# The expert stage of a hybrid decoder layer: one stream of expert pairs becomes two streams that share the array

## What is computed

```python
def hier_moe(h, w_group, b_group, w_router, b_router, w_gate, w_up, w_down):
    pg = softmax(hf @ w_group + b_group)               # 4 groups
    g_val, g_idx = lax.top_k(pg, 1)                    # the best group
    pe = softmax(logits of the 8 experts of that group)
    e_val, e_idx = lax.top_k(pe, 2)                    # its two best experts
    combine = one_hot(expert) * g_val * e_val / sum(e_val)
    a = einsum('btd,edf->btef', h, w_gate)             # w_gate, w_up: 32 x 1024 x 256, f32
    u = einsum('btd,edf->btef', h, w_up)
    z = silu(a) * u * combine
    return einsum('btef,efd->btd', z, w_down)          # w_down: 32 x 256 x 1024, f32
```

## Time and profile before

| | us |
|---|---|
| three runs | 690.07, 686.41, 688.15; median 688.15 |
| span of the profiled execution (its own time beside it isn't given) | 683.7 |
| TensorE matmul busy | 543.3 (79%) |
| TensorE weight loads busy | 274.8 (40%) |
| VectorE busy | 230.6 (34%) |
| GpSimd busy | 178.0 (26%) |
| ScalarE busy | 151.6 (22%) |
| DMA, mean over the span | 247 GB/s |

### The profile page before, as it was taken

One profiled execution on the slowest core, in us unless ns is written; L12 is line 12 of the kernel. 1 busy time (PEld: TensorE's weight loads), 2 busy tenths in 40 slices (PEclk: granted clock), 3 DMA queues, 4 the chain that ended last, 5 costly groups with the idle time before them and its releaser, 6 DMA issues.

```text
span 683.7 us, 7215 instructions
## 1 busy us (share of the span) xinstructions
PE 543.3 (79%) x2420; PEld 274.8 (40%) x2421; DVE 230.6 (34%) x530; ACT 151.6 (22%) x312; POOL 178.0 (26%) x204
## 2 busy tenths in 40 slices
PE   2639999999988799954049989989999979789470
PEld 1328777787534344313023333333333323233120
DVE  0421444232494477785301111111111101011295
ACT  1211444624565012211011111111111101011021
POOL 4200001000543464364531112112212111111075
PEclk9959999999899899986559999999999989999785
DMA  8991855500846802107649976539999999995611
GB/s 288 387 384 30 271 215 185 184 5 6 299 205 230 309 22 105 61 4 275 278 145 402 424 303 247 202 117 417 420 419 420 420 419 420 417 379 198 251 53 73
DMA packets 46005, 168.98 MB, mean 247 GB/s; under 512 B 13178, under 2 KB 22450, under 8 KB 30590
## 3 DMA queue, kind: packets, MB, share of 16 engines
q1 hardware_dynamic: 36682, 146.48, 54.8%
q0 software_dynamic: 8944, 21.87, 9.0%
q10 hardware_dynamic: 340, 0.09, 0.1%
HBM read 165.18 MB, written 18.32 MB: 268 GB/s over the span
## 4 chain that ended last, share of the span: by engine, by line
PE 57%; DVE 13%; DMA 12%; SPq 8%; issue 5%; ACT 3%; POOL 1%; POOLq 0%; DVEq 0%
PE B L1663 16%; PE B L1415 15%; PE B L1682 7%; DMA wex<-in_w_up 4%; DMA win<-in_w_in 3%; PE B L1579 3%; PE B L1352 3%; SPq L369 3%; SPq L371 2%; SPq L368 2%; PE B L1484 2%; DVE bn L1139 2%; DMA ada<-in_w_ada 2%; DVE yy L1321 1%; PE B L1644 1%
## 5 line engine op out<-in xcount | busy, mean ns | idle before, releaser
L1663 PE MATMUL B<-wex,XT 128*64 128x512 f32 x640 | 152.1, 625 | 18.0 <-DMA wex<-in_w_up 10.0
L1415 PE MATMUL B<-hT,win 128*128 128x256 f32 (+1 forms) x448 | 103.1, 390 | 8.1 <-DMA win<-in_w_in 8.1
L1663 PEld LDWEIGHTS B<-wex,XT 128*64 128x64 f32 x640 | 53.2, 144 | 114.8 <-issue 113.6
L1415 PEld LDWEIGHTS B<-hT,win 128*128 128x128 f32 x448 | 85.6, 193 | 28.2 <-DMA win<-in_w_in 8.6
L1682 PE MATMUL B<-wex,zT 128*64 128x512 f32 x320 | 73.1, 599 | 0.6
L1294 DVE TENSOR_TENSOR z<-silu_g,B 128x256 f32<-128x256 f32 x20 | 8.4, 421 | 162.8 <-ACT silu_g L852 162.8
L621 POOL COPY sidx<-idx_all 128x1 int32 (+1 forms) x20 | 3.6, 181 | 200.7 <-DVE yo L1299 200.7
L1579 PE MATMUL B<-wout,yT 128*128 128x512 f32 x112 | 51.3, 617 | 0.0
L1644 PE MATMUL B<-ident,X 128*128 128x128 f32 x168 | 28.4, 295 | 26.8 <-DMA X<-h_dram,gidx 26.8
L852 ACT ACTIVATE silu_g<-B 128x256 f32<-128x256 f32 x20 | 7.7, 384 | 154.7 <-PE B L1663 154.7
L1299 DVE COPY yo<-B 128x512 f32<-128x512 f32 x20 | 13.8, 692 | 83.1 <-PE B L1682 83.1
(11 more groups left out here) (320 smaller groups left out, 627.9 us busy)
## 6 DMA issues: line engine op xcount, KB each, us to landing
wex<-in_w_gate SPq DMA_DIRECT2D x32, 1024.0 KB, 16.7
wex<-in_w_up SPq DMA_DIRECT2D x32, 1024.0 KB, 19.4
wex<-in_w_down SPq DMA_DIRECT2D x32, 1024.0 KB, 20.8
ada<-in_w_ada SPq DMA_DIRECT2D x12, 1024.0 KB, 9.6
ada<-in_w_ada POOLq DMA_DIRECT2D x12, 1024.0 KB, 7.0
win<-in_w_in SPq DMA_DIRECT2D x7, 1024.0 KB, 13.1
wout<-in_w_out SPq DMA_DIRECT2D x1, 4096.0 KB, 13.4
yy<-y_dram SPq DMA_DIRECT2D x8, 512.0 KB, 6.7
```

The lines of the kernel that those rows point to most:

```text
L1415: last = pe.matmul(B[(q % 2) * 2 + h][:, 0:cn], win[:, n % 3, k, col:col + P], hT[:, k, c0:c0 + cn], start=(k == 0), stop=(k == KD - 1))
L1663: last = pe.matmul(B[2 + j % 2][64 * q:64 * q + 64, :], XT[:, j % 2, k, 64 * q:64 * q + 64], gu[:, :, k, :], start=(k == 0), stop=(k == KD ...
```

## The change

The 32 experts are split into two streams that share each step. Stream A has the experts 0 to 7 one at a time, with WA = 64 rows of one expert in a step; stream B has the other 24 in 12 pairs, with WB = 32 rows of each of the two. A step has one unit of A (an expert) and one of B (a pair), and each stream advances with step counts of its own (`uend`, two scans instead of one). The number of steps is the larger of the two sums; a stream that has ended stays at its last unit with empty rows. The array works in four quarters of 128x32: two with A's expert and its rows 0 to 31 and 32 to 63, two with the pair of B. With the counts above, A's experts take 1 1 1 1 3 2 3 2 steps (14), and B's pairs 1 1 1 1 1 2 2 2 1 1 1 1 (15).

Each stream has two places for its weights (`wA0`, `wA1`; `wB0`, `wB1`), so TensorE has four arms for a step instead of three, `arm = 2 * (A's unit odd) + (B's unit odd)`, and each has twice the products of f32 data in quarters (32 for gate/up, 16 for down). TensorE's code of a turn is written out once instead of three times, in one loop over all TURNS (now 11, as MAXSTEP is 44), and each step has an `If` of its own. ScalarE, VectorE and GpSimd keep the three forms, with the `If` per step in the last. SP's loop over pairs becomes a list written out by hand (LOADS). Before the steps, A0, A1 are loaded early, B0 after the stores of x1, then B1.

VectorE's arithmetic for slots, places and needs grows by some operations (64 or 32 rows per step, depending on the stream). GpSimd makes the numbers of steps as one row instead of a grid. The needs of the semaphores and the final waits of GpSimd follow.

Cut to its core (the rest is the arithmetic of slots on VectorE, and the same `one(i, j, ...)` with its `If` on the other engines):

```diff
-CAP = 64
-NPAIR = NE // 2
-
-MAXSTEP = (2 * NT + (CAP - 1) * NPAIR) // CAP
+NA, NB = EPG, (NE - EPG) // 2
+NU = NA + NB
+WA, WB = 64, 32
+
+MAXSTEP = max((2 * NT + (WA - 1) * NA) // WA, (2 * NT + (WB - 1) * NB) // WB)
 RING = 4
 AHEAD = RING - 1
 TURNS = (MAXSTEP + RING - 1) // RING
-MINTURNS = NPAIR // RING
+MINTURNS = max(NA, NB) // RING
...
-        SETS = 3
-        wex = [row("wex0", [P, 2, EXW], "r", 0), row("wex1", [P, 2, EXW], "r", 8 * EXW), row("wex2", [P, 2, EXW], "x", 0)]
+        wA = [row("wA0", [P, 1, EXW], "r", 0), row("wA1", [P, 1, EXW], "r", 4 * EXW)]
+        wB = [row("wB0", [P, 2, EXW], "x", 0), row("wB1", [P, 2, EXW], "r", 8 * EXW)]
...
+        LOADS = [("A", 2), ("B", 2), ("A", 3), ("B", 3), ("B", 4), ("A", 4), ("B", 5), ("A", 5), ("B", 6), ("B", 7),
+                 ("A", 6), ("B", 8), ("A", 7), ("B", 9), ("B", 10), ("B", 11)]
...
-            for q in range(2):
-                load_expert(q, 0, q)
+            for i in range(2):
+                load_a(i)
...
-            sp.wait_ge(lgT_ps, 2)
-            load_expert(2, 1, 0)
+            sp.wait_ge(x1_stored, 16 * (TT + 1))
+            load_b(0, 0)
+            load_b(0, 1)
             sp.wait_ge(lg_ps, 1)
             sp.wait_ge(h2_stored[0], 16 * (TT // 2 + 1))
             sp.wait_ge(h2_stored[1], 16 * (TT // 2))
-            load_expert(3, 1, 1)
-
-            sp.wait_ge(x1_stored, 16 * (TT + 1))
-            load_expert(4, 2, 0, (True, False))
+            load_b(1, 0)
             sp.wait_ge(X_in[AHEAD - 1], 16)
...
+            load_b(1, 1)
...
+            for kind, i in LOADS:
+                before = (i - 2) if kind == "A" else NA + i - 2
+                last_step = sp.value_load(uend_i[0:1, before:before + 1], min_val=1, max_val=MAXSTEP)
                 for half, done in enumerate((gu_ps, y_ps)):
                     sp.wait_ge(done, last_step)
-                    for q in range(2):
-                        load_expert(2 * SETS * i + (2 * j + q), j, q, (half == 0, half == 1))
-
-            with sp.Fori(1, NPAIR // SETS) as i:
-                for j in range(SETS):
-                    load_pair(i, j)
-            for j in range(NPAIR % SETS):
-                load_pair(NPAIR // SETS, j)
-
-            last_step = sp.value_load(pend_i[0:1, NPAIR - 2:NPAIR - 1], min_val=1, max_val=MAXSTEP)
+                    parts = (half == 0, half == 1)
+                    if kind == "A":
+                        load_a(i, parts)
+                    else:
+                        load_b(i, 0, parts)
+                        load_b(i, 1, parts)
...
-            def turn(i, peeled):
-
-
-                for j in range(RING):
-                    n = RING * i + j
-                    place = pe.value_load(place_i[0:1, bass.ds(n, 1)], min_val=0, max_val=SETS - 1)
-                    need = pe.value_load(wneed[0:1, 0, bass.ds(n, 1)], min_val=64, max_val=64 * NPAIR)
-                    need_down = pe.value_load(wneed[0:1, 1, bass.ds(n, 1)], min_val=80, max_val=32 * NPAIR + 48)
-                    for pl in range(SETS):
-                        with pe.If(place == pl):
+            def lanes(a, b):
+
+                return [wA[a][:, 0, :], wA[a][:, 0, :], wB[b][:, 0, :], wB[b][:, 1, :]]
+
+            def one(i, j):
+                n = RING * i + j
+                arm = pe.value_load(arm_i[0:1, bass.ds(n, 1)], min_val=0, max_val=3)
+                need_a = pe.value_load(wneed[0:1, 0, bass.ds(n, 1)], min_val=32, max_val=16 * NA)
+                need_b = pe.value_load(wneed[0:1, 1, bass.ds(n, 1)], min_val=64, max_val=32 * NB)
+                for a in range(2):
+                    for b in range(2):
+                        with pe.If(arm == 2 * a + b):
                             pe.wait_ge(XT_v, n + 1)
                             pe.wait_ge(XT_a, n + 1)
-                            pe.wait_ge(w_in[pl], need)
+                            pe.wait_ge(wA_in[a], need_a + ADA)
+                            pe.wait_ge(wB_in[b], need_b + ADA)
                             for k in range(KD):
-                                for q in range(2):
-                                    gu = wex[pl][:, q, 0:GU].rearrange("p (c k f) -> p c k f", c=2, k=KD)
-                                    last = pe.matmul(B[2 + j % 2][64 * q:64 * q + 64, :], XT[:, j % 2, k, 64 * q:64 * q + 64],
+                                for g, w in enumerate(lanes(a, b)):
+                                    gu = w[:, 0:GU].rearrange("p (c k f) -> p c k f", c=2, k=KD)
+                                    last = pe.matmul(B[2 + j % 2][32 * g:32 * g + 32, :], XT[:, j % 2, k, 32 * g:32 * g + 32],
                                                      gu[:, :, k, :], start=(k == 0), stop=(k == KD - 1))
                             last.then_inc(gu_ps, 1)
                             pe.wait_ge(X_in[(j + 1) % RING], 16 * i + 16 + (16 if j == RING - 1 else 0))
@@ -1671,29 +1703,27 @@
                             last.then_inc(zT_ps, 1)
                             transpose_X((j + 1) % RING, i, 1)
                             pe.wait_ge(zT_ready, n + 1)
-                            if not (peeled and j == 0):
-                                pe.wait_ge(y_v, n)
-                                pe.wait_ge(y_a, n)
-                            pe.wait_ge(down_in[pl], need_down)
+                            pe.wait_ge(y_v, n + 1)
+                            pe.wait_ge(y_a, n + 1)
+                            pe.wait_ge(dA_in[a], need_a)
+                            pe.wait_ge(dB_in[b], need_b)
                             for k in range(2):
                                 for c in range(2):
-                                    for q in range(2):
-                                        dn = GU + k * D + c * 512
-                                        last = pe.matmul(B[5 + c][64 * q:64 * q + 64, :], zT[:, k, 64 * q:64 * q + 64],
-                                                         wex[pl][:, q, dn:dn + 512], start=(k == 0), stop=(k == 1))
+                                    dn = GU + k * D + c * 512
+                                    for g, w in enumerate(lanes(a, b)):
+                                        last = pe.matmul(B[5 + c][32 * g:32 * g + 32, :], zT[:, k, 32 * g:32 * g + 32],
+                                                         w[:, dn:dn + 512], start=(k == 0), stop=(k == 1))
                             last.then_inc(y_ps, 1)
 
             pe.wait_ge(steps_ready, 1)
             pe.wait_ge(X_in[0], 16)
             transpose_X(0, 0, 0)
             transpose_X(0, 0, 1)
-            turn(0, True)
-            with pe.Fori(1, MINTURNS) as i:
-                turn(i, False)
-            nturns = pe.value_load(turns[0:1, 0:1], min_val=MINTURNS, max_val=TURNS)
-            with pe.Fori(MINTURNS, TURNS) as i:
-                with pe.If(nturns > i):
-                    turn(i, False)
+            nsteps = pe.value_load(steps_i[0:1, 0:1], min_val=RING * MINTURNS, max_val=MAXSTEP)
+            with pe.Fori(0, TURNS) as i:
+                for j in range(RING):
+                    with pe.If(nsteps > RING * i + j):
+                        one(i, j)
 
```

More of the change, by code:

```diff
@@ L846, in copy_XT, with one @@
                 act.activation(XT[:, s % 2, 4:8, :], B[1][:, :].rearrange("p (k m) -> p k m", m=P), ACT.Copy).then_inc(XT_a, 1)
-            def turn(i, peeled):
-                for j in range(RING):
-                    n = RING * i + j
[L851 to L865, removed]
+            def one(i, j, first):
+                n = RING * i + j
+                act.wait_ge(gu_ps, n + 1)
+                act.activation(silu_g[:, :], B[2 + j % 2][:, 0:DE], ACT.Silu).then_inc(silu_done, 1)
+                act.wait_ge(zT_ps, n + 1)
+                act.activation(zT[:, :, :], B[4][:, 0:2 * P].rearrange("p (k m) -> p k m", m=P), ACT.Copy).then_inc(zT_ready, 1)
+                copy_XT(j + 1, n + 1)
+                act.wait_ge(y_ps, n + 1)
+                if not first:
+                    act.wait_ge(y_out[j], 16 * i)
+                act.activation(yo[:, j, 512:D], B[6][:, :], ACT.Copy).then_inc(y_a, 1)
+            copy_XT(0, 0)
+            for j in range(RING):
+                one(0, j, True)
+            with act.Fori(1, MINTURNS) as i:
+                for j in range(RING):
+                    one(i, j, False)
+            nsteps = act.value_load(steps_i[0:1, 0:1], min_val=RING * MINTURNS, max_val=MAXSTEP)
             with act.Fori(MINTURNS, TURNS) as i:
-                with act.If(nturns > i):
-                    turn(i, False)
+                for j in range(RING):
+                    with act.If(nsteps > RING * i + j):
+                        one(i, j, False)
             def xhat2(t, n):
@@ L1240, in _ @@
[L1240 to L1244 removed]
+            step(dve.tensor_scalar(unum_i[:, 0, 0:NA], B[5][:, 0:NA], 1.0, float(WA - 1), ALU.max, ALU.add))
+            link(dve.tensor_reduce(umax[:, NA:NU], B[5][:, NA:NE].rearrange("p (a b) -> p a b", b=2), AX.X, ALU.max))
@@ L1276, in _ @@
```

(25 more changed lines are left out.)

187 lines of the change are left out of this document (94 added, 93 removed).

## The result

The changed kernel takes 988.29 us (median of 4 runs, 985.90 to 990.72) where the kernel before takes 687.28 us (4 runs, 686.30 to 690.07): 1.4385 times the time, 95% interval 1.4339 to 1.443, so 301 us slower. Forecast were 859 us and at most 940.

The account below looks back on a forecast made before the run. The prediction saw TensorE's array as busiest, with DMA full from about 460 to 605 us. Span 683.7 + 58 (stage) + 112 (exit) + 1 (VectorE) = 855 us, with 4.5 us to the median 859 us; range 690 to 940 us.

Parts of the forecast that it names:

- the 8 blocks taken as what is held: TensorE's code store: 128 KiB in blocks of 16 KiB, so 8 blocks stay and the new 14.6-block turn does not.
- The jumps back: TensorE's turn loop: on each of three jumps back the first block is fetched again, 15 us in all.
- The walk along the loads alone: Expert stage timed by the weight loads and their gates, without other effects: steps 3, 4, 5 late, end at 607 us.
- Hidden are about 2.6 us, the down product of 3.65 us less its issue: Skipped arms between steps: 2.6 us of each code-fetch wait is covered by the down product.
- I take 5.0: Skipped arms between steps: each block not held costs 5.0 us, chosen between 3.4 and 5.8; 111 us in all.
- at 3.4 us (the queues are empty then) that is 126 us: TensorE leaving its loop: 37 places not held at 3.4 us each, 126 us, of which 112 us show.
- packets in pairs less than 2 us apart: Sign in TensorE's code queue that the prediction is wrong, because code is fetched ahead.
- The other engines' bodies are a few instructions per step: nothing.: Leaving the loop on engines other than TensorE: no added time.
- That the code stays: Rival: TensorE holds 15 blocks or more, only turn 1 pays; 664 to 675 us, 15 in 100.
- That the exit costs nothing: Rival: chains of arms cost, but exit jumps reach blocks that stay; 747 us, 12 in 100.
- fetching ahead of the jumps: Rival: several blocks fetched at once, chains cost a third and the exit half; about 750 us, 8 in 100.
- Tiles that don't overlap: Rival: four narrow array tiles don't overlap, each step 10.7 us longer, 160 us; 2 in 100.

Follow-up runs that it names:

- the step written once: The changed kernel with TensorE's exit edit, plus its step written once instead of four times and single XT and gate/up bank: 681.25 us.
- pairs, 20 steps: The kernel before, 687.28 us; where code doesn't stay, the same with 96 never-executed array instructions added to each arm, 820.24 us.
- exit of TensorE mended: The changed kernel with one more comparison around all four steps of a turn in TensorE's loop: 817.53 us.
- the one with reversed arms: The changed kernel with TensorE's exit edit, plus the four arms written in reverse order in every second step: 809.67 us.
- the last kernel: The kernel with TensorE's step written once, plus one comparison per turn on the other three engines and GpSimd's final counts read before its last loop: 669.82 us.

## Why the prediction was right and wrong

**Right.** The mechanism: code that doesn't stay, arms skipped in series, an exit through far jumps. A table of four kernels shows the first of these, in us (those of the right column are single runs, and the step written once also differs in its single XT):

| | code stays | code doesn't stay |
|---|---|---|
| pairs, 20 steps | 687 | 820 |
| two streams, 15 steps, exit of TensorE mended | 681 | 818 |

Right were also the 8 blocks taken as what is held, the order of the gaps (0.30 us where no arm is skipped, 25 us where six are), over 100 packets, the step's body (12.7 us: 398.2 us of stage less 177.8 of gaps and 30.4 of lower clock, by 15), the narrow tiles, B0's arrival, and that slow steps cover the loads. The jumps back were priced at 5 us each; against the means by skipped arms, the six of the kernel after and the one with reversed arms cost from 1.3 us less to 12.2 more, 5.3 on average. The walk along the loads alone, 607 us, is near the 613.9 us of the last kernel, where code costs least, and in part that is luck. It has the late weights of steps 4 and 5 (413 and 441 us, measured 421.5 and 447.9). From step 5 to step 15 both take 152 us, but the walk by 12.5 us a step and 27 us of waits for weights, the kernel by steps of 15.2 us on average with no such wait.

**Wrong: sizes.** The sum missed the span by 132 us, in two halves.

- *The stage*, forecast to end at 690 us, ended at 755.7. The terms that failed are "Hidden are about 2.6 us, the down product of 3.65 us less its issue" and, less, "I take 5.0". The prediction has 28.5 blocks for the skips, 3 for the jumps back and one late block inside an arm, 32.5 at about 5 us, less 2.6 us in each of 12 gaps: 131 us (111, 15 and 5). The trace has 177.8 us of gaps with 33 packets in them. So the count held; a block cost 5.4 us, 13 us more in all; and the 31 us of cover weren't there. In the first gap five packets make 25.19 us, with nothing left to take off. Six skipped arms were 25.2 and 27.8 us where the prediction has 19.4, four 13.0 to 15.9 (10.4), three 3.8 and 7.7 (5.9), two 4.5 to 7.4 (1.4). With them 13 instead of ten gate/up parts behind a gap ran slow at the lower clock, 28 us (the sum of their durations less 7.1 each) where 17 stood, and step 1 began at 357.54, 4.6 us later than taken, 1.64 of it "issue" with one packet of code in it.
- *The exit*, "at 3.4 us (the queues are empty then) that is 126 us", was 190.5 us. The count of 37 places was right, the price of a place wasn't: 3.4 us is the spacing of single packets, and most places fetch two blocks. The view of the queues from 845 to 895 us of the kernel after has nothing else in it, and its rate in 40 slices of 1.25 us shows each packet (13 GB/s is one of 16 KB in a slice, 26 are two):

```profile
GB/s 13 0 0 13 0 0 26 0 0 13 13 0 0 0 26 0 0 0 26 0 0 13 0 0 13 0 0 13 13 0 0 26 0 0 0 26 0 0 0 26
...
q8 instruction: 20, 0.33, 4.1%
```

The packets go out two at a time, about 4 slices or 4.9 us from pair to pair, four pairs in each turn that isn't run, and two single ones 3 slices or 3.7 us apart: 10 packets and 27 us for five places. The single ones agree with the 3.4 us; a place with a pair costs 4.9. I take the pair for the block jumped to and the one behind it; no run here shows which blocks they are. The prediction's reading that the next block is fetched only once the one ahead is entered doesn't hold here, and "packets in pairs less than 2 us apart" stood among its signs of being wrong. That sign came true at the exit, but without the saving that its rival expected, as the next jump goes 3.6 blocks on, past the second block.

Two results in the prediction don't follow from its terms. With 3.4 and 5.8 us a block they put the stage's end at about 640 and 715 us, not 646 and 731, and the upper end at about 907 us, not 935: further still from the 988 us measured.

**Wrong: a step left out.** "The other engines' bodies are a few instructions per step: nothing." GpSimd's way out of its last loop took 13.2 us on the path to the read of y. In the changed kernel TensorE's exit hid them; the first kernel in which it was mended showed them (21.6 us instead of 10.1), and the last took 9 us back. The place was right in the prediction's sum only because a worse one covered it.

**The rivals.** That the code stays (664 to 675 us) fell for the changed kernel: 140 packets. Yet its time is what the change gives when its premise is made true: 669.82 us. That the exit costs nothing (747 us) fell with 75 packets there, and fetching ahead of the jumps fell with gaps that grow with every skipped arm. Tiles that don't overlap fell with the 7.0 us. A gap of the stage without transfers in the queues wasn't tried. Single packets at the exit are 3.7 us apart and a block in the stage cost 5.4, so the weights' traffic may be some 2 us of it (an estimate); that stays open. So does a computed jump to the arm in place of the chain of comparisons, which wasn't measured.

## What to carry to other kernels

Count the blocks of code between the top and the bottom of a loop before you write out one more arm: up to about 6.7 blocks a loop was fetched once and cost 6 us at most (one run), and 144 instructions more cost this kernel 64 us. Choosing among long arms by a chain of comparisons fetches each arm that is passed over; put the comparison around the small part that differs, or round the whole turn where the turn may not run, and read the queue of code next to the "issue" pieces of the chain. In a sum of waits, take nothing off for what might hide them unless a row shows it: 2.6 us taken off twelve times was the largest single error of the stage here. And ask of each price what a place needs: the spacing of single packets was laid on jumps that fetch two.

## What was not expected of the hardware

- A jump over 3.6 blocks fetches two blocks almost at once and takes about 4.9 us with idle DMA queues. I had expected one block and 3.4 us.
- The edge is sharp: 31 packets and 692 us at about 6.7 blocks a turn, 51 and 756 at about 7.3, 67 and 820 at more than 10.
- The Trainium skill (Runtime: NRT & Kernel Launch, "Instruction fetch mechanics") calls the crossing of a block's border mostly hidden. In the straight code ahead of 343 us the trace agrees: nine packets there in the kernel before (27 less the 12 and 6 of the earlier trace rows), and a single "issue" wait of TensorE, 0.96 us. At the first pass through a turn, where arms are skipped, it was up to 2.1 us, and along a chain of skipped arms 5 us for each. It also says that kernels prefer full unrolling where possible: here the step written once (681 us) beats the four written-out steps (818 us) on the same streams.
- Leaving a loop isn't free on an engine that is nearly idle: GpSimd needed 13.2 us for it, and 3.8 us with one comparison for each turn left over and the reads ahead of the loop.
